# Expert weights as 1 MB pieces, each awaited and refilled by itself, in a one-core fp32 encoder step with a top-4-of-32 MoE

## The chip, the cores and the metric

The kernel runs on one core of one Trainium2 chip. The metric is the device time in microseconds (us) of one launch; lower is better. All data is fp32.

## What is computed

288 token rows (256 of a prompt, 32 of a sample) of width 1024 go through one layer: an adaLN-modulated norm, a combined input projection, a pooling mixer and a Conformer convolution, two sigmoid gates, an output projection, and then the mixture of experts, where nearly all the bytes are:

```python
logits = (t @ router_w + router_b).astype(jnp.float32)
top_vals, top_idx = lax.top_k(logits, TOP_K)              # TOP_K = 4 of N_EXPERTS = 32
top_w = jax.nn.softmax(top_vals, axis=-1)
combine = jnp.sum(one_hot(top_idx, N_EXPERTS) * top_w[..., None], axis=1)
for e in range(N_EXPERTS):
    gt = jnp.minimum(t @ exp_w_gate[e] + exp_b_gate[e], SWIGLU_LIMIT)
    up = jnp.clip(t @ exp_w_up[e] + exp_b_up[e], -SWIGLU_LIMIT, SWIGLU_LIMIT)
    act = gt * jax.nn.sigmoid(SWIGLU_ALPHA * gt) * (up + 1.0)
    out = out + combine[:, e:e + 1] * (act @ exp_w_down[e] + exp_b_down[e])
```

Each of the three matrices of an expert is 1024 x 1024 in fp32, so 4 MB (MB in this text is 1,048,576 bytes for a size of a weight or a transfer; the GB/s of the profile count 10^9 bytes). An expert is 12 MB, the 32 experts 384 MB.

## The kernel before

**The front.** 46 pieces of 1 MB or less (modulation, input projection, gates, pool, convolution and output weights) pass through `ring`, a buffer of 12 slots of 1 MB: 128 partitions with 8 KB each. SyncE (SP) issues all of them in the order of the list `FRONT`. Piece f goes into slot f mod 12 and is issued when the semaphore `piece_used` says that the piece that was in the slot has been multiplied (lines 443 to 447). The pieces of kind "ada" have rows of 8 KB per partition; those of kind "gate" have eight runs of 1 KB per partition.

**The expert loop.** Tokens are sorted on the chip into *items*: up to 64 slots of tokens of one expert. An expert with more than 64 token slots has more than one item. Here there are 33 items for 32 experts, so one expert has two. For each item TensorE (`item`, line 1709) makes three products with the weights as the moving operand: gate (weights in 4 slots), up (4 slots) and down (4 slots). Between them it adds back the results of the item before (`scatter`, lines 1675 and 1662), gathers the tokens of the next item (line 1593, 1601 to 1607) and transposes the activations (line 1722). One product (`product`, line 1627) is 16 pairs of matmuls at line 1642, two 64-column tiles for each of 8 blocks of rows k.

**Where the weights lie.** 16 places of 1 MB: the 12 slots of `ring` and two pairs in `arena` (`EARLY_PAIR`, `LATE_PAIR`) that come free at the end of the front. Before the change they are used in pairs. One transfer, `load` at line 453, brings 2 MB: 128 partitions with one run of 16 KB each, half of one matrix. An expert is 6 transfers (`PER_EXPERT`), and transfer q goes to pair q mod 8. Each pair has one semaphore (`pair_ld`), on which TensorE waits at k = 0 and k = 4 of a product.

**The order of the transfers.** SP issues them all, in the order of use. The first 8 (16 MB, one expert and a third) are issued while the front still runs, each when both slots of its pair are free of front pieces (`front_use`), one of the arena pairs after `logit_mm`. From then on `refill` (line 475) takes them one by one: it waits until `piece_used` says that both 1 MB halves of the pair are multiplied, and issues the transfer that follows eight places later. `piece_used` is counted by TensorE per 1 MB (12 per item, `PIECES`); the threshold is built from `base_i`, a table in a register of the first item of every expert, so that an expert with two items gives its weights up only during its last item.

**The end.** After the last weights SP issues two loads of `mod_rows` (the gate vector g2 spread over the partitions, line 488) and one of `final_g`, in the same queue behind the weights. VectorE needs g2 (line 1211) before it multiplies the sum of the experts (line 1217), adds it to x (line 1220), adds the last item (lines 1235 and 1239), and norms and stores the result.

Of the kernel before, what the change touches and what calls it, by code (L numbers as in the profile page):

```python
# [38 lines left out]
E = 32  # L39
# [17 lines left out]
RING = 12  # L57
SLOT = 2 * D
PIECES = 12
PAIRS = 8  # L60
PER_EXPERT = 6

FRONT = ([("scale", 0, j) for j in range(4)] + [("in", c, 0) for c in (4, 2)]
         + [("shift", 0, j) for j in range(4)] + [("in", c, 0) for c in (5, 3, 0, 1)]
# [3 lines left out]
N_FRONT = len(FRONT)  # L68
F_END = -(-N_FRONT // RING) * RING
USES = [len([f for f in range(N_FRONT) if f % RING == s and FRONT[f][0] != "none"]) for s in range(RING)]  # L70
# [12 lines left out]
def build(nc, x_prompt, x_sample, state_pool, state_conv, c_prompt, c_sample, norm1_g, norm2_g, final_g,  # L83
# [3 lines left out]
    with ExitStack() as ctx:  # L87
# [3 lines left out]
        def sem(name):  # L91
            return ctx.enter_context(nc.semaphore(name))
# [115 lines left out]
        def slots(q, k):  # L208

            if q < RING:  # L210
                return ring[:, q:q + k, :].rearrange("p s n -> p (s n)")
            at = (EARLY_PAIR, LATE_PAIR)[(q - RING) // 2] + SLOT * (q % 2)
            return arena[:, at:at + SLOT * k]
# [2 lines left out]

        slot_ld = [sem(f"slot_ld{s}") for s in range(RING)]
        far_ld = [sem(f"far_ld{i}") for i in range(2)]
        pair_ld = slot_ld[0:RING:2] + far_ld  # L220
        piece_used = sem("piece_used")
        ysb_zero = sem("ysb_zero")
        x_ld = [sem(f"x_ld{t}") for t in range(TT)]
# [146 lines left out]
        wg_v = exp_w_gate[0].rearrange(rows_of, h=2, r=4)  # L370
        wu_v = exp_w_up[0].rearrange(rows_of, h=2, r=4)
        wd_v = exp_w_down[0].rearrange(rows_of, h=2, r=4)
# [19 lines left out]
        def front_piece(f):  # L392

            kind, a, b = FRONT[f]
            slot = ring[:, f % RING, :]
            if kind in ("scale", "shift"):
                at = D if kind == "scale" else 0
                return wada_pv[:, 2 * b:2 * b + 2, at:at + D], slot.rearrange("p (k n) -> p k n", k=2)
            if kind == "ada":
                return wada_v[b][:, 4 * HALF * a:4 * HALF * (a + 1)], slot  # L400
            if kind in ("in", "gate"):
                src = win_v if kind == "in" else gate_v
                return src[:, :, 256 * a:256 * (a + 1)], slot.rearrange("p (k n) -> p k n", k=KD)
            if kind == "pool":
                return poolw_v, slot[:, 0:D].rearrange("p (k n) -> p k n", k=CT)
            if kind == "conv":
                return convw_v[:, :, HALF * a:HALF * (a + 1)], slot.rearrange("p (k n) -> p k n", k=CT)
            return (wout_v[:, 4 * a:4 * a + 4, HALF * b:HALF * (b + 1)], slot.rearrange("p (k n) -> p k n", k=4))
# [28 lines left out]
        @block.sync  # L437
        def _(sp):
            for t in range(2):
                sp.dma_start(x[:, t, :], x_prompt[0, P * t:P * (t + 1), :]).then_inc(x_ld[t], 16)  # L440
            sp.dma_start(x[0:NS_TOK, 2, :], x_sample[0]).then_inc(x_ld[2], 16)
            for f in range(N_FRONT):
                if f >= RING:
                    sp.wait_ge(piece_used, f - RING + 1)
                if FRONT[f][0] != "none":
                    src, dst = front_piece(f)
                    sp.dma_start(dst, src).then_inc(slot_ld[f % RING], 16)

            def load(e, q):

                i, p = q % PER_EXPERT, q % PAIRS
                w = (wg_v, wu_v, wd_v)[i // 2]
                sp.dma_start(slots(2 * p, 2), w[e][:, i % 2, :]).then_inc(pair_ld[p], 16)

            def front_use(i):
                return max(f for f in range(N_FRONT) if f % RING in (2 * i, 2 * i + 1)) + 1

            order = sorted(range(PER_EXPERT), key=front_use)
            for i in order:
                if i == order[3]:  # L460

                    sp.wait_ge(act_c_ready, 1)
                    sp.wait_ge(cst_mm, 4)
                    sp.wait_ge(rows_out[1], 64)
                    load(1, PER_EXPERT)
                sp.wait_ge(piece_used, front_use(i))
                load(0, i)
            sp.wait_ge(logit_mm, TT)
            load(1, PER_EXPERT + 1)
            sp.wait_ge(base_ready, 1)  # L470

            def refill(g, qs):

                at = None
                for q in qs:
                    before, i = (q - PAIRS) // PER_EXPERT, (q - PAIRS) % PER_EXPERT
                    if i == 0 or at is None:
                        at = sp.value_load(base_i[0:1, bass.ds(g * 4 + (before + 1), 1)], min_val=1, max_val=MAX_ITEMS)
                    sp.wait_ge(piece_used, at * PIECES + (F_END - PIECES + 2 * i + 2))
                    load(g * 4 + q // PER_EXPERT, q)  # L480

            with sp.Fori(0, E // 4 - 1) as g:
                refill(g, range(PAIRS, PAIRS + 4 * PER_EXPERT))
            refill(E // 4 - 1, range(PAIRS, 4 * PER_EXPERT))
            at = sp.value_load(base_i[0:1, E - 1:E], min_val=E - 1, max_val=MAX_ITEMS)
            sp.wait_ge(piece_used, at * PIECES + (F_END - PIECES + PIECES))
            for gg, r in ((0, P), (1, NS_TOK)):
                sp.dma_start(g2b[0:r, gg, :], mod_rows[1][gg:gg + 1, D:2 * D].broadcast_to([r, D])).then_inc(spread_ld[2], 16)
            sp.dma_start(fgb, final_g.rearrange("(a d) -> a d", a=1).broadcast_to([P, D])).then_inc(fg_ld, 16)
            for i, t in enumerate(LAST_ORDER):  # L490
                sp.wait_ge(y_ready, i + 1)
                dst = y_sample[0] if t == 2 else y_prompt[0, P * t:P * (t + 1), :]
                sp.dma_start(dst, ybuf[0:ROWS[t], t, :]).then_inc(stored, 16)
            sp.wait_ge(stored, 16 * (16 + TT))
# [300 lines left out]
        def _(dve):  # L795
# [125 lines left out]
            for i, (src, c0, _, _) in enumerate(out_rows):  # L921
                v.transpose(out_stage[i].rearrange("p (c n) -> p c n", c=CT), src[:, :, c0:c0 + 32]).then_inc(out_ev, 1)
# [339 lines left out]
        def _(pe):  # L1262
# [92 lines left out]
            for n in range(12):  # L1355
                f = first_of[("in", (4, 2, 5, 3, 0, 1)[n // 2])]
                w = front_piece(f)[1]
# [31 lines left out]
                elif n == 3:  # L1389

                    pe.wait_ge(shift_ready, 2)
                    for m in range(2):
                        w = front_piece(first_of[("in", (4, 2)[m])])[1]
                        for k in range(KD):
                            q = k % 4
# [22 lines left out]
            for n in range(2 * KD):  # L1418
                f = first_of[("gate", n // 2)]
                w = front_piece(f)[1]  # L1420
# [47 lines left out]
            f = first_of[("pool", 0)]  # L1468
            w = front_piece(f)[1]
# [18 lines left out]
            for m in range(KD):  # L1488
                f = first_of[("conv", m // 4)]
                w = front_piece(f)[1]  # L1490
# [14 lines left out]
            def piece(hh, k):  # L1505
                f = first_of[("out", 0)] + 2 * hh + k // 4
                front_ready(pe, f)
                return front_piece(f)[1][:, k % 4, :]
# [27 lines left out]
            for k in range(KD):  # L1536
                pe.wait_ge(merged_ready, k + 1)
                for q in range(4):
                    w = piece(q // 2, k)
# [92 lines left out]
            def product(out, lhs, g, j, c0, done, mid=None, before_used=None):  # L1632

                for k in range(KD):
                    s = c0 + k // 2
                    if k % 4 == 0:
                        q = PER_EXPERT * j + s // 2
                        used = USES[2 * (q % PAIRS)] if 2 * (q % PAIRS) < RING else 0
                        pe.wait_ge(pair_ld[q % PAIRS], g * 48 + 16 * (used + q // PAIRS + 1))
                    w = slots((PIECES * j + s) % (2 * PAIRS), 1)  # L1640
                    for hh in range(2):
                        ins = mm(out[64 * hh:64 * hh + 64, :], lhs(k), w[:, D * (k % 2) + HALF * hh:D * (k % 2) + HALF * (hh + 1)],  # L1642
                                 start=(done is y_mm and k == 0), stop=(done is y_mm and k == KD - 1) or k == KD - 1,
                                 skip_group_check=True)
                        if k == 0 and hh == 0 and before_used:
                            ins.then_inc(before_used, 1)
                    if k % 2 and k != KD - 1:
                        ins.then_inc(piece_used, 1)
                    if k == 3 and mid:
                        mid()  # L1650
                ins.then_inc(done, 1)
# [125 lines left out]
```

## Time and profile before

| | |
|---|---|
| median of 3 runs | 1179.45 us (1175.89 to 1179.46) |
| the profiled execution: time, span | 1179.84 us, 1177.8 us |
| TensorE busy, weight loads busy | 1135.3 us (96%), 451.5 us (38%) |
| VectorE, ScalarE, GpSimd busy | 474.4, 199.2, 33.4 us |
| DMA traffic | 456.11 MB (10^6), mean 387 GB/s |
| chain that ended last | PE 74%, DMA 22%, DVE 3% |

The span is the profiler's, from the first to the last record of the execution; the time is the device's, 2.0 us more. The busy time of TensorE holds pipelined matmuls whose ends are modelled, so 96% busy is not 96% of its peak. "DMA" in the profile's slices and stretches is the busy share of the core's 16 DMA engines, by the time that their packets took; it can read slightly over 1. The granted clock column (PEclk) is 1.00 when TensorE runs at its full 2.4 GHz.

### The profile page before, as it was taken

What the parts mean: (1) busy time and instruction counts of PE and PEld (TensorE: products, weight loads), DVE (VectorE), ACT (ScalarE), POOL (GpSimd) and SP (SyncE); (2) the same over time, 40 slices, a digit from 0 to 9 for tenths busy, and PEclk for the clock granted to TensorE, in tenths of its full rate; (3) what the DMA queues carried; (4) which work ended last, traced back from release to release, by engine and by line L of the source; (5) the groups of instructions that cost most, each with busy time, mean ns of one, the idle gap of its engine ahead of it and who ended that gap; (6) DMA issues with size and microseconds to landing.
All of it is one profiled execution on the core that took longest, in us unless ns stands there. A gap on an engine that the chain in (4) does not pass through costs nothing.

```text
span 1177.8 us, 15962 instructions
## 1 busy us (share of the span) xinstructions
PE 1135.3 (96%) x5938; PEld 451.5 (38%) x5939; DVE 474.4 (40%) x1082; ACT 199.2 (17%) x365; POOL 33.4 (3%) x81
## 2 busy tenths in 40 slices
PE   8999999899999999999999999999999999999993
PEld 5676675533333333333333333333333333333330
DVE  3398424643333333333333333333333333333337
ACT  2001301311111111111111112111111111111112
POOL 4002300100000000000000000000000000000000
PEclk8999999999999999999999999999999999999997
DMA  9977687589999999999999999999999999999992
GB/s 345 370 265 275 252 303 275 213 332 425 428 428 428 428 427 428 428 428 430 429 428 428 372 410 428 429 428 428 429 427 428 428 429 428 428 429 428 429 426 86
DMA packets 55211, 456.11 MB, mean 387 GB/s; under 512 B 6949, under 2 KB 21857, under 8 KB 28565
## 3 DMA queue, kind: packets, MB, share of 16 engines
q1 hardware_dynamic: 51392, 452.87, 92.8%
q10 hardware_dynamic: 3797, 2.95, 1.0%
q8 instruction: 14, 0.23, 0.1%
q14 instruction: 8, 0.07, 0.0%
HBM read 454.40 MB, written 1.40 MB: 387 GB/s over the span
## 4 chain that ended last, share of the span: by engine, by line
PE 74%; DMA 22%; DVE 3%; issue 0%; SPq 0%; ACT 0%; ACTq 0%; DVEq 0%
PE bank L1642 43%; DMA ring<-in_exp_w_gate 14%; DMA arena<-in_exp_w_gate 6%; PE bank L1427 5%; PE bank L1675 4%; PE bank L1375 4%; PE bank L1593 4%; DMA ring<-mod_rows 2%; PE bank L1513 2%; PE bank L1722 1%; PE bank L1497 1%; PE bank L1601 1%; PE bank L1349 1%; PE bank L1662 1%; PE bank L1295 1%; PE bank L1605 1%
## 5 line engine op out<-in xcount | busy, mean ns | idle before, releaser
L1642 PE MATMUL bank<-ring,arena 128*64 128x512 f32 x2368 | 530.1, 597 | 13.4 <-DMA ring<-in_exp_w_gate 11.7
L1642 PEld LDWEIGHTS bank<-ring,arena 128*64 128x64 f32 x2368 | 162.5, 137 | 354.1 <-issue 312.9
L1642 PE MATMUL bank<-arena 128*64 128x512 f32 x800 | 179.3, 596 | 3.3 <-DMA arena<-in_exp_w_gate 3.3
L1190 DVE TENSOR_SCALAR arena<-bank 128x512 f32<-128x512 f32 x33 | 22.8, 691 | 295.0 <-PE bank L1642 295.0
L1175 DVE TENSOR_TENSOR arena<-arena,bank 128x512 f32<-128x512 f32 x132 | 84.8, 684 | 110.9 <-PE bank L1675 79.4
L762 ACT ACTIVATE arena<-arena 32x256 f32<-32x256 f32 x136 | 56.0, 412 | 432.0 <-DVE arena L1119 430.8
L1642 PEld LDWEIGHTS bank<-arena 128*64 128x64 f32 x800 | 54.8, 137 | 117.9 <-issue 106.7
L1675 PE MATMUL bank<-arena 64*128 64x512 f32 x264 | 74.5, 641 | 0.0
L1593 PE MATMUL bank<-h,arena 128*64 128x512 f32 x272 | 64.4, 593 | 0.2 <-DVE arena L1042 0.2
L1427 PE MATMUL bank<-arena,ring 128*128 128x288 f32 x256 | 64.4, 409 | 0.0
L775 ACT ACTIVATE arena<-arena 128x512 f32<-128x512 f32 x33 | 20.8, 630 | 207.6 <-DVE arena L1190 207.6
L904 DVE SCALAR_TENSOR_TENSOR h<-h,arena 128x318 f32<-128x318 f32 x120 | 55.5, 538 | 0.0
L1427 PEld LDWEIGHTS bank<-arena,ring 128*128 128x128 f32 x256 | 48.1, 190 | 17.1 <-issue 4.2
L1197 DVE TENSOR_SCALAR arena<-bank 128x512 f32<-128x512 f32 x33 | 22.8, 691 | 75.9 <-PE bank L1642 75.9
L1375 PE MATMUL bank<-arena,ring 128*128 128x288 f32 x192 | 49.5, 418 | 0.0
L775 ACT ACT_TABLE_LOAD x33 | 42.3, 1283 | 0.6
L1375 PEld LDWEIGHTS bank<-arena,ring 128*128 128x128 f32 x192 | 37.2, 195 | 12.8 <-issue 2.5
L782 ACT ACTIVATE arena<-bank 128x512 f32<-128x512 f32 x33 | 19.7, 598 | 131.8 <-PE bank L1642 131.8
L1675 PEld LDWEIGHTS bank<-arena 64*128 64x128 f32 x264 | 19.9, 184 | 53.6 <-issue 53.6
L1605 PE MATMUL bank<-biases,mine 32*64 32x288 f32 x264 | 40.0, 414 | 0.0
L1122 DVE COPY arena<-arena 32x256 f32<-32x256 f32 x136 | 38.3, 282 | 2.6
L1607 PE MATMUL bank<-h,arena 32*64 32x512 f32 x136 | 37.4, 613 | 0.0
(297 smaller groups left out, 750.8 us busy)
## 6 DMA issues: line engine op xcount, KB each, us to landing
ring<-in_exp_w_down SPq DMA_DIRECT2D x48, 2048.0 KB, 26.7
ring<-in_exp_w_gate SPq DMA_DIRECT2D x48, 2048.0 KB, 24.1
ring<-in_exp_w_up SPq DMA_DIRECT2D x48, 2048.0 KB, 25.6
arena<-in_exp_w_gate SPq DMA_DIRECT2D x16, 2048.0 KB, 23.1
arena<-in_exp_w_up SPq DMA_DIRECT2D x16, 2048.0 KB, 28.1
arena<-in_exp_w_down SPq DMA_DIRECT2D x16, 2048.0 KB, 26.7
ring<-in_w_ada SPq DMA_DIRECT2D x24, 1024.0 KB, 10.2
ring<-in_gate_w SPq DMA_DIRECT2D x8, 1024.0 KB, 6.7
```

The costliest lines, as they stand in the source:

```text
L762: ins = a.activation(*square_moves(1, s, u), ACT.Copy)
L775: a.activation(gsig, gmin, ACT.Sigmoid, scale=ALPHA).then_inc(gsig_ready, 1)
L904: ins = v.scalar_tensor_tensor(out=yc[:, c, :], in0=uc_ext[:, c, k:k + CW], scalar=tap, in1=yc[:, c, :], op0=ALU.mult, op1=ALU.add)
L1122: ins = v.tensor_copy(*square_moves(0, s, u))
L1175: ins = v.tensor_tensor(acc[:, t, cs], acc[:, t, cs], bank[6 + hh][:, :], ALU.add)
L1375: ins = mm(bank[n % 4][:, 0:TOK], w[:, k, P * (n % 2):P * (n % 2 + 1)], (hS if n < UNSHIFTED else hT)[:, k, :], start=(k == 0), stop=(n >= ...
L1427: ins = mm(bank[n % 4][:, 0:TOK], w[:, k, P * (n % 2):P * (n % 2 + 1)], hT[:, k, :], start=(k == 0), stop=(k == KD - 1))
L1593: ins = mm(bank[0][64 * hh:64 * hh + 64, :], oh[:, t, :], half_rows(h2[:, t, :], hh), start=start, stop=stop, skip_group_check=True)
L1605: found = mm(bank[6 + i][out, 0:TOK], mine[LOOKUP, :], routedT[:, i, :], start=True, stop=True, skip_group_check=True)
L1607: ins = mm(bank[0][out, :], oh[0:NS_TOK, 2, :], half_rows(h2[0:NS_TOK, 2, :], hh), start=start, stop=stop, skip_group_check=True)
L1642: ins = mm(out[64 * hh:64 * hh + 64, :], lhs(k), w[:, D * (k % 2) + HALF * hh:D * (k % 2) + HALF * (hh + 1)], start=(done is y_mm and k == ...
L1675: ins = mm(bank[6 + hh][:, :], ohwT[64 * hh:64 * hh + 64, P * t:P * (t + 1)], ysb[64 * hh:64 * hh + 64, :], start=True, stop=True, skip_gr ...
```

## The change

A transfer of expert weights is now 1 MB, 8 KB per partition, into one slot. There are 12 per expert and 16 places, each with its own semaphore (`place_ld`: the 12 of the ring and 4 new ones). TensorE waits at k = 0, 2, 4 and 6 of a product, each time for 1 MB. `refill` waits for one piece and reloads one slot. The first 16 MB are now 16 transfers, each issued when its one slot is free.

```diff
-PAIRS = 8
-PER_EXPERT = 6
+PLACES = 16
...
-        far_ld = [sem(f"far_ld{i}") for i in range(2)]
-        pair_ld = slot_ld[0:RING:2] + far_ld
+        far_ld = [sem(f"far_ld{i}") for i in range(4)]
+        place_ld = slot_ld + far_ld
...
             def load(e, q):
-                i, p = q % PER_EXPERT, q % PAIRS
-                w = (wg_v, wu_v, wd_v)[i // 2]
-                sp.dma_start(slots(2 * p, 2), w[e][:, i % 2, :]).then_inc(pair_ld[p], 16)
+                i, p = q % PIECES, q % PLACES
+                w = (wg_v, wu_v, wd_v)[i // 4]
+                sp.dma_start(slots(p, 1), w[e][:, i % 4 // 2, SLOT * (i % 2):SLOT * (i % 2 + 1)]).then_inc(place_ld[p], 16)
 
             def front_use(i):
-                return max(f for f in range(N_FRONT) if f % RING in (2 * i, 2 * i + 1)) + 1
-
-            order = sorted(range(PER_EXPERT), key=front_use)
+                return max(f for f in range(N_FRONT) if f % RING == i) + 1
+
+            order = sorted(range(PIECES), key=front_use)
             for i in order:
-                if i == order[3]:
+                if i == order[6]:
...
-                    load(1, PER_EXPERT)
+                    load(1, PIECES)
+                    load(1, PIECES + 1)
...
-            load(1, PER_EXPERT + 1)
+            load(1, PIECES + 2)
+            load(1, PIECES + 3)
...
                 for q in qs:
-                    before, i = (q - PAIRS) // PER_EXPERT, (q - PAIRS) % PER_EXPERT
+                    before, i = (q - PLACES) // PIECES, (q - PLACES) % PIECES
...
-                    sp.wait_ge(piece_used, at * PIECES + (F_END - PIECES + 2 * i + 2))
-                    load(g * 4 + q // PER_EXPERT, q)
+                    sp.wait_ge(piece_used, at * PIECES + (F_END - PIECES + i + 1))
+                    load(g * 4 + q // PIECES, q)
...
                 for k in range(KD):
                     s = c0 + k // 2
-                    if k % 4 == 0:
-                        q = PER_EXPERT * j + s // 2
-                        used = USES[2 * (q % PAIRS)] if 2 * (q % PAIRS) < RING else 0
-                        pe.wait_ge(pair_ld[q % PAIRS], g * 48 + 16 * (used + q // PAIRS + 1))
-                    w = slots((PIECES * j + s) % (2 * PAIRS), 1)
+                    q = PIECES * j + s
+                    if k % 2 == 0:
+                        used = USES[q % PLACES] if q % PLACES < RING else 0
+                        pe.wait_ge(place_ld[q % PLACES], g * 48 + 16 * (used + q // PLACES + 1))
+                    w = slots(q % PLACES, 1)
```

SP's instructions at the start of the expert loop, before (the first refill of the loop, gate weights used, up weights of the next expert loaded; "waits" names the semaphore):

```order
L453 ISA [waits piece_used]
L453 DMA ring<-in_exp_w_up 128x4096
L479 REGISTER_ALU
L453 ISA [waits piece_used]
L453 DMA ring<-in_exp_w_up 128x4096
L479 REGISTER_ALU
L453 DMA ring<-in_exp_w_down 128x4096 [waits piece_used]
```

and in the changed kernel:

```order
L452 ISA [waits piece_used]
L452 DMA ring<-in_exp_w_up 128x2048
L480 REGISTER_ALU
L452 ISA [waits piece_used]
L452 DMA ring<-in_exp_w_up 128x2048
L480 REGISTER_ALU
L452 ISA [waits piece_used]
L452 DMA ring<-in_exp_w_up 128x2048
L480 REGISTER_ALU
L452 ISA [waits piece_used]
L452 DMA ring<-in_exp_w_up 128x2048
```

Each transfer of 4096 fp32 per partition has become two of 2048, with a wait of its own; nothing is reordered. TensorE's first product of the loop, before:

```order
L1642 MATMUL bank<-ring,arena 64x512 [waits slot_ld0]
L1642 MATMUL bank<-ring,arena 64x512 x7
L1639 REGISTER_ALU
L1642 MATMUL bank<-ring,arena 64x512 [waits slot_ld2]
L1642 MATMUL bank<-ring,arena 64x512 x7
```

and in the changed kernel:

```order
L1643 MATMUL bank<-ring,arena 64x512 [waits slot_ld0]
L1643 MATMUL bank<-ring,arena 64x512 x3
L1643 MATMUL bank<-ring,arena 64x512 [waits slot_ld1]
L1643 MATMUL bank<-ring,arena 64x512 x3
L1640 REGISTER_ALU
L1643 MATMUL bank<-ring,arena 64x512 [waits slot_ld2]
L1643 MATMUL bank<-ring,arena 64x512 x3
L1643 MATMUL bank<-ring,arena 64x512 [waits slot_ld3]
L1643 MATMUL bank<-ring,arena 64x512 x3
```

The matmuls are the same ones in the same order; there are four waits where there were two.

## Rows read from the trace of the kernel before

**Rows 1.** The page: DMA share and GB/s in 40 slices; one issue row
```profile
DMA  9977687589999999999999999999999999999992
GB/s 345 370 265 275 252 303 275 213 332 425 428 428 428 428 427 428 428 428 430 429 428 428 372 410 428 429 428 428 429 427 428 428 429 428 428 429 428 429 426 86
...
ring<-in_exp_w_gate SPq DMA_DIRECT2D x48, 2048.0 KB, 24.1
```
**Rows 2.** Stretches: us, PE, PEld, DVE, ACT, POOL busy (count), PEclk, DMA, GB/s
```profile
300.00:600.00 300.00, 296.11 (x1558) 98.02 (x1556) 103.47 (x228) 49.64 (x87) 0.00 (x0) 1.00 1.01 428
700.00:1140.00 440.00, 430.50 (x2252) 141.13 (x2250) 149.80 (x331) 73.13 (x128) 0.00 (x0) 1.00 1.01 428
```
**Rows 3.** The chain of waits, 1080 to 1178 us: start us, us, what
```profile
1092.97 33.13 DMA ring<-in_exp_w_gate
...
1127.63 25.75 DMA ring<-mod_rows
...
1154.70 3.48 DVE arena L1217 x3
```
**Rows 4.** The chain of waits, 600 to 700 us, one item without a stall
```profile
644.78 13.88 PE bank L1642 x64
...
672.07 13.88 PE bank L1642 x64
```
**Rows 5.** Timeline of PE: start us, us, engine, line, op, count, idle before and releaser
```profile
539.59 3.65 PE L1642 MATMUL bank<-ring,arena 128*64 128x512 f32 x16 [0.58 <-DMA ring<-in_exp_w_gate]
...
627.72 2.79 PE L1642 MATMUL bank<-ring,arena 128*64 128x512 f32 x12 [1.24 <-DMA ring<-in_exp_w_gate]
...
984.14 3.65 PE L1642 MATMUL bank<-ring,arena 128*64 128x512 f32 x16 [1.25 <-DMA ring<-in_exp_w_gate]
```
**Rows 6.** Stretches of the front in which pieces of kind "ada" land
```profile
97.00:101.00 4.00, 4.00 (x20) 2.76 (x22) 4.00 (x10) 0.62 (x2) 0.00 (x0) 1.00 1.02 416
107.00:111.00 4.00, 4.00 (x23) 2.69 (x25) 3.97 (x9) 0.62 (x2) 0.44 (x1) 1.00 1.02 424
117.00:121.00 4.00, 4.00 (x21) 2.86 (x23) 2.86 (x4) 1.04 (x3) 3.63 (x6) 1.00 0.98 410
127.00:131.00 4.00, 4.00 (x18) 2.98 (x16) 2.31 (x2) 3.41 (x4) 2.09 (x5) 1.00 1.02 420
```
**Rows 7.** DMA packets by size, from 107 to 111 us, then from 300 to 600 us
```profile
DMA packets 223, 1.70 MB, mean 424 GB/s; under 512 B 16, under 2 KB 16, under 8 KB 16
...
DMA packets 8822, 128.45 MB, mean 428 GB/s; under 512 B 982, under 2 KB 982, under 8 KB 982
```
**Rows 8.** Stretches at the start of the loop
```profile
235.00:241.00 6.00, 6.00 (x26) 1.92 (x24) 3.93 (x20) 1.86 (x2) 0.00 (x0) 0.85 0.36 93
241.00:246.00 5.00, 5.00 (x30) 1.37 (x26) 2.70 (x5) 0.63 (x1) 0.00 (x0) 1.00 0.92 390
...
261.00:266.00 5.00, 5.00 (x27) 1.60 (x24) 0.10 (x1) 1.88 (x2) 0.00 (x0) 1.00 0.95 354
```
**Rows 9.** Timeline of SP, 210 to 296 us: start, us, issue
```profile
224.09 0.33 SPq L453 DMA_DIRECT2D ring<-in_exp_w_down  x1
225.62 0.33 SPq L453 DMA_DIRECT2D arena<-in_exp_w_gate  x1
239.05 4.85 SPq L453 DMA_DIRECT2D ring<-in_exp_w_up  x2
```
**Rows 10.** Stretches around the expert with two items
```profile
653.00:660.00 7.00, 7.00 (x40) 2.10 (x36) 0.69 (x1) 1.31 (x2) 0.00 (x0) 1.00 0.68 243
660.00:676.00 16.00, 16.00 (x96) 5.56 (x90) 7.94 (x15) 2.12 (x6) 0.00 (x0) 1.00 1.00 412
676.00:682.00 6.00, 6.00 (x32) 2.00 (x30) 0.97 (x5) 1.88 (x2) 0.00 (x0) 1.00 0.88 330
```
**Rows 11.** Timeline of SP, 590 to 700 us
```profile
655.27 4.81 SPq L453 DMA_DIRECT2D ring<-in_exp_w_up  x2
```
**Rows 12.** Waits of PE's weight loads for DMA: total us, times, longest
```profile
PEld bank L1642 <- DMA ring<-in_exp_w_gate: 25.2, 16, 2.1
```

More of the change, by code:

```diff
@@ L475, in refill @@
                 for q in qs:
-                    before, i = (q - PAIRS) // PER_EXPERT, (q - PAIRS) % PER_EXPERT
+                    before, i = (q - PLACES) // PIECES, (q - PLACES) % PIECES
                     if i == 0 or at is None:
                         at = sp.value_load(base_i[0:1, bass.ds(g * 4 + (before + 1), 1)], min_val=1, max_val=MAX_ITEMS)
-                    sp.wait_ge(piece_used, at * PIECES + (F_END - PIECES + 2 * i + 2))
-                    load(g * 4 + q // PER_EXPERT, q)
+                    sp.wait_ge(piece_used, at * PIECES + (F_END - PIECES + i + 1))
+                    load(g * 4 + q // PIECES, q)
             with sp.Fori(0, E // 4 - 1) as g:
-                refill(g, range(PAIRS, PAIRS + 4 * PER_EXPERT))
-            refill(E // 4 - 1, range(PAIRS, 4 * PER_EXPERT))
+                refill(g, range(PLACES, PLACES + 4 * PIECES))
+            refill(E // 4 - 1, range(PLACES, 4 * PIECES))
             at = sp.value_load(base_i[0:1, E - 1:E], min_val=E - 1, max_val=MAX_ITEMS)
```

## The prediction

> **What bounds the kernel now.** I read the page first: from the tenth slice on, about 265 us, the DMA line shows 9 tenths in every slice and the rate is 428 GB/s, but for two slices near 660 us [rows 1]. The stretches come next. Two things look full at once there: TensorE is busy for 296.11 of 300 us and for 430.50 of 440 us, and the 16 DMA engines for 1.01 of the time, at 428 GB/s in both stretches [rows 2]. Only one can set the end. TensorE is not at its limit: where it does not stall, an item begins every 672.07 - 644.78 = 27.3 us [rows 4], while the 12 MB (12.58 million bytes) of an expert take 29.4 us at 428 GB/s. So TensorE is 2.1 us per expert too fast for the queue. It starts the loop with 16 MB in store, uses that lead up (the first stall is at 539.59 us, and after the expert with two items has refilled the store the next is at 984.14 us), and from there waits up to 1.2 us at a time for gate weights, and its weight loads up to 2.1 us [rows 5, 12]. Those waits are the queue's pace, not a cost of their own. The chain of waits confirms the end: 33 us of DMA, and then 25.75 us of the load of `mod_rows`, which lies in the queue behind the last weights; VectorE's closing work starts on it [rows 3]. The reader should see that the end of the kernel is the time at which the queue has moved its last byte, plus some 24 us of closing work that the change does not touch. What counts is therefore (a) how fast the DMA engines move the bytes, and (b) how long they stand idle after the front.
>
> **(a) The pace of the queue.** 184 of the 192 transfers of 2 MB land after the loop's first store, 386 million bytes; at 428 GB/s that is 901 us. They now come as 8 KB rows instead of 16 KB rows, two packets in place of one, and one more completion packet per MB and engine. The trace of before has the same shape of transfer: the front's "ada" pieces are 1 MB with 8 KB per partition. Four stretches of 4 us hold them back to back: 416, 424, 410 and 420 GB/s [rows 6]. That they are pure is seen in the packet counts: from 107 to 111 us only 16 packets of 223 are under 8 KB, and these are completions, as the 982 of 8822 in the loop are [rows 7]. In such a short stretch a packet more or less at its edges is 1%, so I look from both sides. The best of the four, 424, is 0.9% under 428: +8.5 us. Their mean, 417.5, is 2.5% under: +23 us. By packets: 207 of 8 KB at share 1.02 of 16 engines over 4 us is 315 ns for one; in the loop 7840 of 16 KB at share 1.01 over 300 us is 618 ns; two of the small against one of the large is 1.9% longer. I take **1.7%, +15.3 us**, the middle of the two ends and just under the count of packets, because the front's stretches also carry small transfers of other queues. It is paid in full, since the queue is the bound: nothing covers it, and TensorE's spare 2.1 us per expert grows to 2.6 us.
>
> Here the Trainium skill speaks against the change more loudly. "DMA: Bandwidth & Descriptors", section Bandwidth, gives 341 GB/s for a transfer of 1 MB and 425 GB/s for one of 16 MB, and a rule to batch to 1 MB or more; an estimate by that row would put the 386 million bytes at 1132 us, some 230 us more. The trace disagrees: 1 MB transfers with others queued behind them run at 410 to 424 GB/s [rows 6], so the fixed part is hidden by the queue, and the sum goes by the rows.
>
> **(b) The idle time.** Nothing before about 235 us moves. The first 16 MB are still issued at the same thresholds: the last steps are at 224.09 and 225.62 us [rows 9], where both slots of a pair come free by one increment. A few single slots are issued earlier, but the queue is empty again before the loop in either case (it is at 235 us [rows 8]), so this gives nothing; I bound it by 0 and 0.5 us. Then:
> - Start of the loop. The engines run dry at about 235 us and restart after the first refill, at 239.05 us; six us at 93 GB/s and the two later dips [rows 8] are 4.7 + 0.4 + 0.9 = 6.0 us of lost queue time. The first refill waits for k = 0 to 3 of the first product. Released after k = 0 and 1 it is issued 1.8 to 2.5 us earlier (half of the time from 234 to 239 us). The pieces after it are used unevenly, so some of it is given back. I take **-2 us**, bounds 0 and -4.
> - The expert with two items. Its weights are held for two items; the queue runs out at 653 to 656 us and dips again at 676 to 682 us. Lost: 7 x (1 - 243/428) = 3.0 us, 16 x (1 - 412/428) = 0.6 us, 6 x (1 - 330/428) = 1.4 us, 5.0 us together [rows 10]. The refill that ends it is at 655.27 us [rows 11], after k = 3 of the second item's gate product; a quarter of a product is 1.8 us (half a product, 16 matmuls, takes 3.65 us [rows 5]), so it comes at 653.5 us, as the store runs out. The second dip has the same cause with the down product. I take **-2 us**, bounds 0 and -4.
> - SP issues 6 transfers more per expert at 0.33 us each [rows 9]. It has 12 x 0.33 = 4 us to spend per 29.9 us and is 24 us ahead, the median from issue to landing [rows 1]. Nothing.
> - TensorE has 6 more waits per item. Where the semaphore is already there they could cost some tens of ns each, under 1 us per item, beside 2.6 us of spare. If that spare were gone they would be on the path; it is not.
> - At the end TensorE waits for the last 1 MB instead of the last 2 MB and so finishes 1.8 us sooner after it. But VectorE's closing work starts on `mod_rows`, behind that same MB in the queue, and then needs 7 us before it wants TensorE's last result [rows 3]. Nothing.
>
> **Sum**: 1179.84 (this execution's own time; span 1177.8 and 2.0 around it) + 15.3 - 2 - 2 = 1191.1, rounded to **1191 us**. The median of the runs shown, 1179.45, is 0.4 us lower, which is within their spread.
>
> **The rivals.**
> 1. *Finer refills win, the row size costs nothing* (other side). Mechanism: SP's waits at the start of the loop and in the double item are the only idle time of the queue, 6.0 + 5.0 = 11 us [rows 8, 10], and half-size pieces recover about 4, at most 8 of it, while packets of 8 KB are overlapped by the engines so well that the pace stays 428 GB/s. Time 1176, down to 1172. It decides if the loss of pace is below 0.44% (4 us of 901). For it: one stretch of four reaches 424 in 4 us, where edges alone could hide 1%. Against: none of the four reaches 428, and the packet count says 1.9%. Chance 0.08.
> 2. *A small loss of pace that the regained idle time cancels*: 0.5 to 0.8%, +4.5 to +7 us against -4. Time 1180 to 1183, within 0.3%. Chance 0.10. 
> 3. *TensorE's waits are the cost, so the finer waits gain*: in the last 200 us and from 540 to 650 us its weight loads stall up to 2.1 us per item [rows 5, 12]; who takes these for a cost of 2 MB granularity expects them halved, some 20 us less, 1160 us. Against: the queue is at 428 GB/s in just these stretches [rows 2], so a stall saved would need bytes that are not there. Chance 0.02.
> 4. *The pace falls by 2.5% or more*, by the worst rows (417.5 to 410 GB/s), or single rows of 8 KB out of 16 KB are read less well from HBM than whole ones: +23 to +39 us, less 4: 1199 to 1215. Chance 0.12.
> The rest, 0.68, is the forecast, 1184 to 1199.
>
> **How the numbers follow.** A measurement of this kernel tells about 0.3% (3.5 us) from no change. Slower: 0.68 + 0.12 = 0.80, and of the second rival's upper edge 0.01, 0.81; same 0.09; faster 0.08 + 0.02 = 0.10. The range goes from the bound of 0.9% with 4 us regained (1184), one us lower for the regained time, to 2.5% with the same (1199): 1183 to 1199.
>
> **What would show it.** Right: in 300 to 600 us the DMA share stays at 1.0 and the rate is 418 to 423 GB/s; twice as many packets of 8 KB or more; TensorE's stalls for DMA grow in total (first one at about 450 us, not 540); the first refill issued near 236.5 us; 653 to 660 us well above 243 GB/s; the chain still ends with `mod_rows`. Wrong: 427 to 428 GB/s (rival 1), or a DMA share clearly below 1.0 in mid-loop, which would mean that SP or `piece_used` had become the bound, something no term here has.

## The result, and the profile after

The changed kernel takes 1186.8 us (median of 4 runs, 1185.91 to 1188.44) against 1179.45 us (4 runs, 1175.89 to 1180.56). The ratio is 1.0069 with a 95% interval of 1.0045 to 1.0093: slower by 0.7%. The profiled execution has a span of 1184.4 us and a time of 1186.27 us; that of before had 1177.8 and 1179.84. So 6.6 us of span are to be found.

Page of the changed kernel, the DMA share, the rate and the packets, and an issue row [rows 1]:

```profile
DMA  9977686599999999999999999999999999999992
GB/s 343 371 261 285 254 338 222 213 382 421 420 422 421 421 422 422 422 421 423 422 422 421 422 421 422 422 422 421 422 422 421 421 423 421 421 422 422 422 421 87
...
ring<-in_exp_w_gate SPq DMA_DIRECT2D x96, 1024.0 KB, 24.8
```

Two things differ from before. The loop stands at 421 to 422 GB/s, not 428. And the notch of before near 660 us (372 and 410 GB/s) is gone. The stretches of the changed kernel say the same in numbers [rows 2, 8, 10], with the columns of the rows of before, and so does, in the second fence, the count of its packets from 300 to 600 us [rows 7]:

```profile
300.00:600.00 300.00, 296.83 (x1558) 97.34 (x1554) 103.27 (x227) 49.65 (x87) 0.00 (x0) 1.00 1.01 421
700.00:1140.00 440.00, 429.66 (x2236) 138.31 (x2228) 147.77 (x328) 72.49 (x127) 0.00 (x0) 1.00 1.01 422
226.00:300.00 74.00, 71.25 (x380) 24.20 (x370) 32.73 (x95) 17.09 (x28) 1.27 (x1) 0.98 0.97 397
640.00:700.00 60.00, 60.00 (x330) 20.38 (x328) 21.27 (x45) 9.14 (x16) 0.00 (x0) 1.00 1.01 422
```

```profile
DMA packets 17357, 126.44 MB, mean 421 GB/s; under 512 B 1925, under 2 KB 1925, under 8 KB 1925
```

For the two stretches that were not shown of before, the same view of the kernel before:

```profile
226.00:300.00 74.00, 71.25 (x378) 24.16 (x368) 32.52 (x94) 17.18 (x28) 1.26 (x1) 0.98 0.94 386
640.00:700.00 60.00, 60.00 (x330) 20.37 (x328) 21.73 (x46) 9.14 (x16) 0.00 (x0) 1.00 0.95 392
```

In 300 us of full queue the changed kernel moves 126.44 MB where before moved 128.45 MB [rows 7]: 1.6% less with the DMA engines as busy (share 1.01). On 901 us of queue time that is **+14.3 us**. The time that the queue lost in a stretch is its length times one minus its rate over the full rate (428 before, 421.5 after). From 226 to 300 us: 7.3 us before, 4.3 after, **-3.0 us**. From 640 to 700 us, where the expert with two items holds its weights: 5.0 us before, nothing after, **-5.0 us**. The sum, +6.3 us, leaves 0.3 of the 6.6 us unexplained. (The prediction counted 6.0 us at the start, from three short stretches; over the whole stretch from 226 to 300 us it is 7.3.)

SP's timeline of the changed kernel shows the first refill at 237.44 us, where it was 239.05 [rows 9], and the first refill of the double item at 654.65 us, where it was 655.27 [rows 11]:

```profile
237.44 6.13 SPq L452 DMA_DIRECT2D ring<-in_exp_w_up  x4
...
654.65 6.53 SPq L452 DMA_DIRECT2D ring<-in_exp_w_up  x4
```

TensorE's waits for DMA, changed kernel [rows 12], and the closing part of its chain of waits [rows 3]:

```profile
PEld bank L1643 <- DMA ring<-in_exp_w_gate: 37.6, 30, 1.4
PEld bank L1643 <- DMA ring<-in_exp_w_up: 15.4, 24, 0.8
```

```profile
1136.18 23.71 DMA ring<-mod_rows
1161.22 3.48 DVE arena L1218 x3
```

The weight loads wait for gate weights more often and longer in total (37.6 us in 30 waits where it was 25.2 in 16), each wait shorter (1.4 us at most where it was 2.1). The first experiment below, with rows of 8 KB but waits in pairs, has 34.0 us in 19 waits, 2.2 at most: so most of the rise in the sum comes from the slower queue, and the shorter single wait from the finer grain. A wait of an engine that is faster than its feed only measures the feed. The end still hangs on `mod_rows`, behind the last weights: it lands at 1159.9 us, where it was 1153.4 [rows 3], and 24.5 us of closing work follow, where it was 24.4. So 6.5 of the 6.6 us lie before that landing.

TensorE's first stall in the loop, changed kernel, against 539.59 us before [rows 5]:

```profile
540.93 1.94 PE L1643 MATMUL bank<-ring,arena 128*64 128x512 f32 x8 [0.48 <-DMA ring<-in_exp_w_gate]
```

One thing changed that the times do not show. SP's issues of `down` weights, before and then after (count, then the least, median and longest time of one in ns):

```profile
L453 SPq DMA_DIRECT2D ring<-in_exp_w_down x48: 328/333/341, 163.2 to 1086.7; - x48
L452 SPq DMA_DIRECT2D ring<-in_exp_w_down x96: 328/1664/6248, 153.6 to 1100.8; - x96
```

An issue of these weights, which always took a third of a microsecond, now takes up to 6.2 us. The long ones lie mostly where TensorE stalls, so that nearly all 16 MB are on order: from 560 to 640 us the 30 issues take 67 us together. From 640 to 700 us, where the double item has held its weights, each of the 20 takes 0.33 us again. The pace is 421 to 422 GB/s in both, so this costs nothing here, but SP has next to no time left over where the issues are long.

### The profile page after: what moved, and what is told of

Its sections match the earlier page's. It is cut to its first block, busy times and chain, and to the rows that moved or that the text cites. A ratio compares the mean times of both kernels' runs of the same rounds, so it can differ in the third digit from the quotient of the medians.

```text
span 1184.4 us, 16576 instructions
## 1 busy us (share of the span) xinstructions
PE 1141.6 (96%) x5938; PEld 449.7 (38%) x5939; DVE 474.8 (40%) x1082; ACT 199.2 (17%) x365; POOL 33.4 (3%) x81
## 4 chain that ended last, share of the span: by engine, by line
PE 75%; DMA 19%; DVE 3%; SPq 2%; issue 1%; ACT 0%; ACTq 0%; DVEq 0%
PE bank L1643 45%; DMA ring<-in_exp_w_gate 14%; PE bank L1428 5%; PE bank L1676 4%; PE bank L1376 4%; PE bank L1594 4%; DMA arena<-in_exp_w_gate 2%; SPq L452 2%; DMA ring<-mod_rows 2%; PE bank L1514 2%; PE bank L1723 1%; PE bank L1498 1%; PE bank L1602 1%; PE bank L1350 1%; PE bank L1663 1%; PE bank L1296 1%
## 5 line engine op out<-in xcount | busy, mean ns | idle before, releaser
L1602 PE MATMUL bank<-biases,mine 32*64 32x512 f32 x136 | 37.4, 613 | 0.0
```

The source lines that it names most:

```text
L1602: mm(bank[3][out, :], mine[B_GATE, :], bias_rows[B_GATE, cs], start=True, stop=False, skip_group_check=True)
```

## The experiments

Two theories and their rivals were open after this: is the lost pace due to the rows, to the number of transfers, or to something in HBM; and what regained the idle time, SP's finer refills, TensorE's finer waits, or something else. The ratios below are against the kernel before, run on the same chip. Each reading of lost time is from one execution.

### Rows of 8 KB alone, everything else in pairs

The edit is to the kernel before.

```diff
-                sp.dma_start(slots(2 * p, 2), w[e][:, i % 2, :]).then_inc(pair_ld[p], 16)
+                for m in range(2):
+                    sp.dma_start(slots(2 * p + m, 1), w[e][:, i % 2, SLOT * m:SLOT * (m + 1)]).then_inc(pair_ld[p], 16)
-                        pe.wait_ge(pair_ld[q % PAIRS], g * 48 + 16 * (used + q // PAIRS + 1))
+                        pe.wait_ge(pair_ld[q % PAIRS], g * 96 + 16 * (used + 2 * (q // PAIRS + 1)))
```

> The kernel before with each 2 MB transfer issued as two transfers of 1 MB with 8 KB rows on the pair's semaphore; refills and waits stay in pairs. My theory (8 KB rows cost pace, single refills regain idle time of the queue): the loop runs at 421 to 422 GB/s as in the changed kernel, the dips at 235 to 241 us and at the expert with two items are back in full (5 us lost around 653 to 690 us), and the time is 1193 us (1190 to 1196), 6 us more than the changed kernel. Rival, that the smaller grain itself (waits of SP or TensorE) costs the time: the pace returns to 428 and the time is 1179.

1190.79 us, ratio 1.0096 (1.0069 to 1.0122), span 1188.6. The stretches of this run:

```profile
226.00:300.00 74.00, 71.25 (x374) 24.29 (x370) 32.85 (x94) 16.87 (x28) 1.27 (x1) 0.98 0.95 387
300.00:600.00 300.00, 294.18 (x1548) 97.08 (x1544) 103.00 (x227) 49.64 (x87) 0.00 (x0) 1.00 1.01 421
640.00:700.00 60.00, 59.94 (x314) 19.84 (x312) 20.62 (x45) 9.14 (x16) 0.00 (x0) 1.00 0.99 400
```

With waits and refills back in pairs the pace is still 421, so the small grain of the waits has no part in it. The dip at the double item is back, but with 60 x (1 - 400/421.5) = 3.1 us, not 5: the slower queue alone takes 1.9 us off it. At the start it loses 6.1 us, where the changed kernel lost 4.3 and before 7.3. The interval of the time's ratio overlaps that of the changed kernel (1.0045 to 1.0093): that the finer waits and refills regain time is read from these stretches, not from the two times.

### Rows of 16 KB, 1 MB per transfer, over half the partitions

The edit is to the kernel before; TensorE's wait counts are those of the last experiment.

```diff
-                sp.dma_start(slots(2 * p, 2), w[e][:, i % 2, :]).then_inc(pair_ld[p], 16)
+                for m in range(2):
+                    ps = slice(64 * m, 64 * m + 64)
+                    sp.dma_start(slots(2 * p, 2)[ps, :], w[e][ps, i % 2, :]).then_inc(pair_ld[p], 16)
```

> The kernel before with each 2 MB transfer issued as two of 1 MB over 64 partitions each, so that rows stay 16 KB while the number of transfers and of completion packets doubles as in the changed kernel. If the cost is per row: pace 427 to 428 GB/s, time 1180 us. If it is per transfer (issue, completion): pace 421 to 422, time 1193. A third outcome, that transfers over half the partitions are slower for a reason of their own, would show as a pace below 420.

2104.73 us, ratio 1.78. This is the third outcome, and far larger than I had thought of:

```profile
300.00:600.00 300.00, 188.22 (x762) 56.25 (x760) 52.03 (x117) 24.90 (x45) 0.00 (x0) 0.82 1.01 212
```

The DMA engines are as busy as ever (1.01) and move 212 GB/s, half of 428. The experiment says nothing on the question it was made for, so it was made again over other partitions.

### The same over the even and the odd partitions

As the last, with the partitions taken in another way.

```diff
-                    ps = slice(64 * m, 64 * m + 64)
-                    sp.dma_start(slots(2 * p, 2)[ps, :], w[e][ps, i % 2, :]).then_inc(pair_ld[p], 16)
+                    sp.dma_start(slots(2 * p, 2)[m:P:2, :], w[e][m:P:2, i % 2, :]).then_inc(pair_ld[p], 16)
```

> As e2 (1 MB transfers over 64 partitions with 16 KB rows, issued in pairs), but over the even and then the odd partitions instead of the lower and then the upper half. If e2's halved pace came from using one half of the partitions, the packets are back at 613 ns and the pace at 427 to 428 GB/s if the cost is per row (time 1180), or 421 to 422 if it is per transfer (time 1191). If 64 partitions of any kind are slow, it stays near 212 GB/s and 2100 us.

1179.68 us, ratio 1.0006 (0.9994 to 1.0018), the first outcome:

```profile
300.00:600.00 300.00, 296.67 (x1562) 98.30 (x1560) 104.32 (x230) 49.64 (x87) 0.00 (x0) 1.00 1.01 428
640.00:700.00 60.00, 60.00 (x332) 20.38 (x330) 21.52 (x46) 9.14 (x16) 0.00 (x0) 1.00 0.96 394
```

Twice the transfers, twice the completion packets, the same 16 KB rows: 428 GB/s. The number of transfers costs nothing here. The 8 KB run in pairs has the same transfers of 1 MB, as many, with the same waits, and rows half as long: 421 GB/s. What costs is the row. Whether its time is spent in the DMA engines or in reading HBM, no run here separates.

### Rows of 4 KB

The edit is to the changed kernel, with the counts of TensorE's waits doubled as above. A transfer is now 0.5 MB, so the number of transfers doubles once more together with that of the rows.

```diff
-                sp.dma_start(slots(p, 1), w[e][:, i % 4 // 2, SLOT * (i % 2):SLOT * (i % 2 + 1)]).then_inc(place_ld[p], 16)
+                for m in range(2):
+                    at = SLOT * (i % 2) + D * m
+                    sp.dma_start(slots(p, 1)[:, D * m:D * (m + 1)], w[e][:, i % 4 // 2, at:at + D]).then_inc(place_ld[p], 16)
```

> The changed kernel with each 1 MB piece in two transfers with rows of 4 KB on its semaphore: the suspected cost per packet doubled again. If a packet costs a fixed time beside its bytes (28.4 us per expert at 16 KB rows against 29.8 at 8 KB rows says about 10 ns), the pace falls to 408 to 410 GB/s and the time is 1214 us (1208 to 1220). If 8 KB rows lost pace for another reason (HBM reads of half rows, the number of transfers in flight), it stays near 420 and the time near 1188.

(The 28.4 us per expert in this text should read 29.4.) 1214.61 us, ratio 1.0282 (1.0251 to 1.0313):

```profile
300.00:600.00 300.00, 291.74 (x1530) 94.34 (x1528) 103.52 (x225) 47.26 (x84) 0.00 (x0) 1.00 1.03 409
640.00:700.00 60.00, 58.59 (x306) 19.06 (x304) 19.20 (x42) 9.13 (x16) 0.00 (x0) 1.00 1.03 410
```

The time per row and engine is 16 x bytes / rate: 612 ns for 16 KB (428.2 GB/s), 311 ns for 8 KB (421.5), 160 ns for 4 KB (409.5). Two rows of 8 KB cost 9.8 ns more than one of 16 KB, two of 4 KB cost 9.1 ns more than one of 8 KB. A fixed 9 to 10 ns per row explains all three; the expectation said about 10. Without it all three sizes would run at some 435 GB/s, an estimate from these three rates. The completion packets have no visible part in it, since the last experiment doubled them at 428 GB/s. The rival of the expectation, that 4 KB rows would stay near 420 GB/s, has fallen.

### SP's refills in pairs, TensorE's waits single

The edit is to the changed kernel.

```diff
-                    sp.wait_ge(piece_used, at * PIECES + (F_END - PIECES + i + 1))
+                    sp.wait_ge(piece_used, at * PIECES + (F_END - PIECES + 2 * (i // 2) + 2))
```

> The changed kernel with SP's refills in pairs again (it waits until both pieces of a pair are used, then issues two transfers of 1 MB); TensorE still awaits single pieces. My theory, that the refills regain the idle time: the dip at the double item returns (3 to 5 us lost), pace 421 to 422, time 1191 us (1189 to 1194). Rival, that TensorE's finer waits regain it: time stays at 1187.

1190.09 us, ratio 1.0082 (1.0055 to 1.0108), span 1190.2:

```profile
226.00:300.00 74.00, 71.91 (x376) 25.15 (x378) 31.74 (x94) 17.59 (x29) 1.61 (x2) 0.95 0.93 380
640.00:700.00 60.00, 60.00 (x314) 19.60 (x312) 20.51 (x45) 9.14 (x16) 0.00 (x0) 1.00 1.00 406
```

Lost: 7.3 us at the start, 2.2 us at the double item. The time is as forecast and the dip smaller than forecast (3 to 5). The 7.3 us at the start are not all due to the edit. This execution began its first product 1.1 us later than the changed kernel's, and at the lower clock for longer: the granted clock from 235 to 241 us is 0.70 on average, so partly at 1.2 GHz, where the changed kernel had 0.89, and the first product took 9.01 us, where it took 8.43.

```profile
235.00:241.00 6.00, 6.00 (x22) 1.72 (x21) 4.21 (x21) 2.90 (x2) 0.00 (x0) 0.70 0.28 117
```

That of the changed kernel:

```profile
235.00:241.00 6.00, 6.00 (x28) 1.88 (x26) 3.85 (x20) 1.78 (x2) 0.00 (x0) 0.89 0.53 173
```

The dip at the double item is free of this: from 640 to 700 us the granted clock is 1.00 in each of the runs of the table below.

### TensorE's waits in pairs, SP's refills single

The edit is to the changed kernel.

```diff
-                    if k % 2 == 0:
-                        used = USES[q % PLACES] if q % PLACES < RING else 0
-                        pe.wait_ge(place_ld[q % PLACES], g * 48 + 16 * (used + q // PLACES + 1))
+                    if k % 4 == 0:
+                        for r in (q, q + 1):
+                            used = USES[r % PLACES] if r % PLACES < RING else 0
+                            pe.wait_ge(place_ld[r % PLACES], g * 48 + 16 * (used + r // PLACES + 1))
```

> The changed kernel with TensorE waiting for both pieces of a pair at k = 0 and 4; SP still refills piece by piece. My theory: TensorE has 2.5 us to spare per expert and the queue stays full, so this costs nothing: 421 to 422 GB/s, no dip at the double item, 1187 us (1185 to 1189). Rival, that finer awaiting is what gained: the time goes up by 3 us or more.

1187.45 us, ratio 1.0076 (1.0051 to 1.0101), span 1184.8:

```profile
226.00:300.00 74.00, 71.56 (x364) 24.24 (x363) 30.81 (x87) 14.82 (x23) 0.00 (x0) 0.95 0.96 389
640.00:700.00 60.00, 60.00 (x322) 20.48 (x326) 21.22 (x46) 9.14 (x16) 0.00 (x0) 1.00 1.00 409
```

The time is as I said, but "no dip at the double item" is wrong: 1.8 us are lost there. The single execution also began its first product 2.6 us earlier than the changed kernel's (230.99 against 233.59 us), so its span is no clean test of the rest, and the intervals of the two times overlap nearly fully. The dip is the sturdier reading: refills and waits both have a share in closing it. A reason that fits, and that no run here singles out: a TensorE that waits for 2 MB starts an item one landing of 1 MB later, and so gives its pieces back later. The trace agrees as far as it goes: the first refill of the double item is out at 655.25 us here and at 654.65 in the changed kernel, which had entered the loop 2.6 us later.

| | rate | lost 226 to 300 us | lost 640 to 700 us | time, ratio |
|---|---|---|---|---|
| before | 428 | 7.3 | 5.0 | 1 |
| 8 KB rows, all in pairs | 421 | 6.1 | 3.1 | 1.0096 |
| 8 KB, refills in pairs | 422 | 7.3 | 2.2 | 1.0082 |
| 8 KB, waits in pairs | 421 | 5.7 | 1.8 | 1.0076 |
| changed kernel | 421 | 4.3 | 0.0 | 1.0069 |

How much of a difference in the columns of lost time is chance can be judged from two other runs here with rows of 16 KB, waits in pairs and refills of 2 MB at the double item: they lose 4.8 us (the even and odd run) and 4.2 us (the run under (a) below), where before lost 5.0. So 0.0 stands far outside of what chance does and 3.1 lies 1.1 under the least of the three, while 3.1, 2.2 and 1.8 differ by little more than chance.

### Finer refills in some places only

The finer grain regains idle time only where the queue runs dry; everywhere else its rows cost. So the kernel before was given finer refills in part.

(a) The first six refills of the loop as two transfers of 1 MB, the first half on a semaphore of its own:

```diff
+        early_ld = slot_ld[1:RING:2]
...
+                    if first and q - PAIRS < PER_EXPERT:
+                        n, p = q % PER_EXPERT, q % PAIRS
+                        w = (wg_v, wu_v, wd_v)[n // 2][q // PER_EXPERT]
+                        for m, done in enumerate((early_ld[q - PAIRS], pair_ld[p])):
+                            sp.wait_ge(piece_used, at * PIECES + (F_END - PIECES + 2 * i + m + 1))
+                            sp.dma_start(slots(2 * p + m, 1), w[:, n % 2, SLOT * m:SLOT * (m + 1)]).then_inc(done, 16)
+                        continue
...
+                        if PAIRS <= q < PAIRS + PER_EXPERT:
+                            pe.wait_ge(early_ld[q - PAIRS], 16 * (USES[2 * (q - PAIRS) + 1] + 1))
```

> The kernel before, in which only the first six refills of the loop are two transfers of 1 MB each, refilled singly; all else is 2 MB with 16 KB rows. Theory: pace 428 GB/s from 300 us on, the idle time at the start of the loop falls from about 7 us to 4 or 5, the dip at the double item stays at 5 us: 1177.5 us (1176 to 1179), 2 to 3 us under the kernel before. Rival, that the start is set by something else than the refills: 1180.

1177.71 us against 1180.01 us, ratio 0.9981 (0.9968 to 0.9994): faster than the kernel before by 0.2%, and so than the changed one. Its own profile does not show where. SP's timeline, and then the stretches:

```profile
236.39 7.75 SPq L485 DMA_DIRECT2D ring<-in_exp_w_up  x4
```

```profile
226.00:300.00 74.00, 71.26 (x364) 24.11 (x362) 31.31 (x88) 16.19 (x27) 0.94 (x1) 0.95 0.96 387
640.00:700.00 60.00, 60.00 (x330) 20.38 (x328) 22.91 (x50) 10.07 (x19) 0.00 (x0) 1.00 0.97 398
```

The first refill is out at 236.39 us, 2.7 us earlier, but by 300 us only 0.2 us more of the queue's time is used than before (7.1 lost, 7.3 before), since in this execution TensorE's first product took 10.05 us, where it took 8.62; the granted clock from 235 to 241 us is 0.69 here, where it was 0.85 [rows 8]. At the double item it loses 4.2 us, and nothing was changed there. The gain of the medians stands, small as it is; that it comes from the start of the loop is not shown.

(b) One refill in six, the one behind the first gate half of each expert, as two transfers of 1 MB, split in the same way. `load` now takes the register `at` and does the waiting for all refills:

```diff
+        half_ld = {0: 1, 2: 5, 4: 9, 6: 3}
...
+                if i == PAIRS % PER_EXPERT:
+                    for m, done in enumerate((slot_ld[half_ld[p]], pair_ld[p])):
+                        if at is not None:
+                            sp.wait_ge(piece_used, at * PIECES + (F_END - PIECES + m + 1))
+                        sp.dma_start(slots(2 * p + m, 1), w[e][:, i % 2, SLOT * m:SLOT * (m + 1)]).then_inc(done, 16)
+                    return
...
+                        if q % PER_EXPERT == PAIRS % PER_EXPERT:
+                            at = half_ld[q % PAIRS]
+                            pe.wait_ge(slot_ld[at], g * 16 + 16 * (USES[at] + 1))
```

> The kernel before, in which of each expert's six refills only the one behind the first gate half is two transfers of 1 MB, refilled singly. Theory: one transfer in six has 8 KB rows, so the pace is 427 GB/s (+2.4 us), while the first dip at the double item (3 us) and about 2 us at the start are regained: net 1177 us (1175 to 1179.5). Rival: the dips only move to the next refill, which is 2 MB, and the time is 1181 to 1182.

1182.09 us, ratio 1.0023 (1.0009 to 1.0036): the rival's outcome. The double item loses 60 x (1 - 397/427) = 4.2 us, as much as under (a), where nothing was changed there. The last three stretches are those of [rows 10]:

```profile
300.00:600.00 300.00, 295.89 (x1558) 98.02 (x1556) 102.83 (x227) 49.64 (x87) 0.00 (x0) 1.00 1.01 427
640.00:700.00 60.00, 60.00 (x332) 20.39 (x330) 21.99 (x47) 9.15 (x17) 0.00 (x0) 1.00 0.98 397
653.00:660.00 7.00, 7.00 (x40) 2.13 (x38) 0.69 (x1) 1.06 (x2) 0.00 (x0) 1.00 0.95 364
660.00:676.00 16.00, 16.00 (x88) 5.53 (x90) 7.93 (x15) 2.06 (x5) 0.00 (x0) 1.00 1.00 385
676.00:682.00 6.00, 6.00 (x30) 2.01 (x28) 0.97 (x5) 1.88 (x2) 0.00 (x0) 1.00 0.88 311
```

The first stretch loses less than before (364 GB/s for 243), the two behind it lose more (385 for 412, 311 for 330). Helping the first refill alone moves the dip to the ones behind it, and the pace pays for it in every expert.

## Why the prediction was right

The forecast was 1191 us in a range of 1183 to 1199; 1186.8 came. The sign and the mechanism hold: the queue is the bound, its row size is paid in full, part is given back as regained idle time, and the end hangs on the queue's last bytes. Step by step:

- **Pace**: +15.3 us forecast (1.7%), +14.3 measured (1.6%). The first rival, that 8 KB rows cost no pace, fell by the 8 KB run in pairs. That the loss goes with the transfers and not with the rows fell by the even and odd run. The page of the Trainium skill, "DMA: Bandwidth & Descriptors", section Bandwidth, whose rate for a 1 MB transfer (a row that the page gives for transfers issued by GpSimd) would have meant, by the prediction's estimate, some 230 us, does not carry over to a queue that is never empty: the even and odd run moves 1 MB transfers at 428 GB/s. The estimate in the Trainium skill's terms, from the same page's "Why small descriptors are slow (HBM only)", 0.6%, has the right form, a fixed cost per packet, but less than half the size of the 1.6% measured.
- **Start of the loop**: -2 us forecast, -3.0 measured in one pair of executions. The first refill came at 237.44 us, not near 236.5: 3.85 us after the product began, where it was 5.37, so 1.5 us sooner and not 1.8 to 2.5. TensorE had waited just before it, and the granted clock from 235 to 241 us is 0.89, so partly at 1.2 GHz: the first quarter of the product took 3.85 us, not the 2.5 or so that the prediction had for it.
- **Double item**: -2 us forecast with a bound of -4, -5.0 measured. This is the term that was mis-sized, and its bound was wrong. I had only moved the first refill forward by a quarter of a product, to 653.5 us; it came at 654.65. Two things were left out: the slower queue empties the store later, which alone takes 1.9 us off the dip (the 8 KB run in pairs; 1.1 against the smallest dip with 16 KB rows), and single refills and single waits shorten both dips, not the first alone (single waits alone take 0.9 us more off, single refills alone 1.3, the two together 3.1; the first two figures are hardly beyond what two executions differ by).
- **Front, TensorE's extra waits, the end**: nothing forecast, and nothing seen. The first product begins at 233.59 us, where it was 233.68. A group of 64 matmuls without a stall takes 13.88 us with its waits doubled, as it did before [rows 4]. The closing work is 24.5 us, where it was 24.4.

```profile
645.88 13.88 PE bank L1643 x64
```

- **SP**: nothing forecast, and the pace bears it out: the share of the DMA engines stays at 1.01. But the working, 12 issues of 0.33 us and so 4 us of every 29.9, is wrong: an issue takes up to 6.2 us, and from 560 to 640 us the issues fill 67 of 80 us. It cost nothing because the queue was full while SP was held.
- **What would show it**: rate 418 to 423 (421 to 422), twice the packets (17357 for 8822), more stalls in total (37.6 us for 25.2), no dip from 653 to 660 us, `mod_rows` at the end: as said. One sign did not come: the first stall was to be at about 450 us, not 540, and it is at 540.93. The 450 has no working behind it. By the prediction's own spare, 2.1 us per expert before and 2.6 after, a store that lasted 306 us of the loop would last 247, to 481 us. The slower queue does bring the stall forward, to 512.28 us in the 8 KB run in pairs, and single waits put it back, to 539.64 us with the refills in pairs. A reason that fits: TensorE then starts on 1 MB less, 2.5 us of the feed, about one expert's spare.

```profile
512.28 3.65 PE L1643 MATMUL bank<-ring,arena 128*64 128x512 f32 x16 [1.04 <-DMA ring<-in_exp_w_gate]
```

With -3.0 and -5.0 in place of -2 and -2, and 14.3 in place of 15.3, the same sum gives 1186.1 for the profiled execution, which took 1186.27.

## What to carry to other kernels

Where a stream of weights is the bound and its queue never empties, a finer transfer cannot save a stall: the consumer's waits measure the feed, and only the feed's rate and its idle time count. Ask first whether the DMA engines are ever idle; the finer grain is worth exactly a part of that (8 of 12 us here), and it costs what shorter rows cost on all the bytes (14 us here). Use the fine grain in the places where the queue runs dry and keep the long rows elsewhere (here a gain of 0.2%, whose place is not shown), and check that the next refill behind it does not inherit the dip.

## What the runs showed of the hardware

- A row costs 9 to 10 ns beside its bytes on each of the 16 DMA engines: 428.2, 421.5 and 409.5 GB/s with rows of 16, 8 and 4 KB. With rows of 16 KB it is 428 GB/s at 1 and at 2 MB per transfer.
- With a full queue of 8 KB rows one issue of a transfer of 1 MB took SP up to 6.2 us, and 0.33 us where the queue had just run low. With rows of 16 KB, the same bytes and as many transfers of 1 MB (the even and odd run), none took more than 1.3 us. So, as far as these runs show, it goes with the number of rows that are waiting and not with that of transfers; at how many rows it begins, none of them shows.
- Transfers of 1 MB over the lower and then the upper 64 partitions run at 212 GB/s, and over the even and then the odd partitions at 428, with the DMA share at 1.01 both times. I had not expected it. The Trainium skill, "DMA: Bandwidth & Descriptors", section The descriptor swizzle, says that in a transfer to 128 partitions, 0 to 63 are written through the even half of the ports and 64 to 127 through the odd half; the halved rate agrees with that, and no run here shows the ports themselves.
- In that run, where TensorE waited for weights for more than a third of the time (188.22 us busy of 300), the granted clock of the stretch from 300 to 600 us is 0.82 on average, so partly at the lower level of 1.2 GHz; before it was 1.00 (2.4 GHz) there, with TensorE busy for 296.11 us [rows 2].
